# Bank waits moved to their tiles, and two norms' transposes set between halves of products, in a two-block transformer kernel

## The reference

```python
# first block
h = h + mixed                       # mixed = concat(...) @ w_out
z = rms_norm(h, ffn_gain) @ w_ff1   # 1024 -> 4096
h = h + square(relu(z)) @ w_ff2     # 4096 -> 1024
# second block
h = rmsnorm(x, norm_mix) * (1 + sc1) + sh1
proj = h @ w_in                     # 1024 -> 8192, then rope, retention, differential attention
x = x + g1 * (merged @ w_out)
x = x + g2 * hierarchical_moe(...)  # 32 experts
```

## Time and profile before

| | |
|---|---|
| median of 3 runs | 1199.39 us |
| the profiled execution's own time | 1197.58 us |
| its span, first to last instruction | 1195.8 us |
| mean granted TensorE clock | 0.987 of full |
| VectorE / ScalarE busy | 566.8 us (47%) / 477.0 us (40%) |
| chain that ended last | TensorE 89%, VectorE 3%, ScalarE 3% |
| DMA queue time, share of 16 engines | 70.6% |

### The profile page before, as it was taken

The page is one execution under the profiler, slowest core; times in us unless marked ns, Lnnn a source line. Parts: engine busy times, 40 slices in busy tenths (PEclk is TensorE's granted clock), DMA queues, the critical chain, the costliest instruction groups (busy, mean ns, idle before and its releaser), DMA issues.

```text
span 1195.8 us, 19252 instructions
## 1 busy us (share of the span) xinstructions
PE 1157.4 (97%) x8093; PEld 890.7 (74%) x8093; DVE 566.8 (47%) x860; ACT 477.0 (40%) x790; POOL 16.2 (1%) x32
## 2 busy tenths in 40 slices
PE   7989999999999999999999999999999999999995
PEld 6968888799988878878888787666666666666663
DVE  5688344677674377477564644222222222222222
ACT  5566133454443354563556524322222232332222
POOL 3000000000000000000000000000000000000000
PEclk9889999999999999999999999999999999999998
DMA  9743769255455555454444479999999999999992
GB/s 318 240 141 129 260 248 344 86 211 198 158 209 188 171 160 184 141 185 145 162 141 141 165 321 373 411 430 428 429 428 429 429 430 429 429 427 429 429 429 105
DMA packets 79823, 332.08 MB, mean 278 GB/s; under 512 B 4236, under 2 KB 6607, under 8 KB 63231
## 3 DMA queue, kind: packets, MB, share of 16 engines
q1 hardware_dynamic: 78356, 328.43, 70.6%
q0 software_dynamic: 1088, 2.34, 0.8%
q10 hardware_dynamic: 298, 0.11, 0.0%
HBM read 329.82 MB, written 1.05 MB: 277 GB/s over the span
## 4 chain that ended last, share of the span: by engine, by line
PE 89%; DVE 3%; ACT 3%; issue 2%; DMA 1%; SPq 1%; ACTq 0%; DVEq 0%
PE bank L1036 19%; PE bank L434 13%; PE bank L436 13%; PE bank L435 13%; PE bank L1055 10%; PE bank L1028 5%; PE bank L552 3%; PE bank L427 2%; DMA ring<-in_w_in 1%; PE bank L1075 1%; DVE arena L1822 1%; PE bank L1076 1%; ACT arena_r L1235 1%; PE bank L1043 1%; SPq L2496 0%
## 5 line engine op out<-in xcount | busy, mean ns | idle before, releaser
L1739 DVE TENSOR_TENSOR ring_r<-ring,arena_r 128x2048 fp32r<-128x2048 f32 x93 | 212.3, 2291 | 164.6 <-ACT arena_r L1235 163.8
L1235 ACT ACTIVATE arena_r<-ring 128x2048 fp32r<-128x2048 f32 x93 | 177.6, 1917 | 201.1 <-PE bank L436 189.8
L436 PE MATMUL bank<-arena_r,actT_r 128*128 128x512 f32 (+1 forms) x400 | 157.3, 393 | 0.0
L434 PE MATMUL bank<-arena_r,tok_r 128*128 128x512 f32 (+1 forms) x368 | 146.6, 398 | 3.3 <-issue 2.3
L435 PE MATMUL bank<-ring_r,tok_r 128*128 128x512 f32 (+1 forms) x368 | 143.4, 390 | 0.0
L2328 DVE TENSOR_TENSOR arena<-bank,arena 64x512 f32<-64x512 f32 x64 | 44.1, 689 | 180.5 <-PE bank L1055 179.8
L434 PE MATMUL bank<-tok_r,arena_r 128*128 128x256 f32 x352 | 99.4, 282 | 2.8 <-DVE ring_r L1751 1.9
L1206 ACT ACTIVATE arena<-bank 128x512 f32<-128x512 f32 (+5 forms) x132 | 57.5, 464 | 110.4 <-PE bank L1043 46.8
L435 PE MATMUL bank<-actT_r,arena_r 128*128 128x256 f32 x352 | 99.6, 283 | 0.0
L436 PE MATMUL bank<-tok_r,ring_r 128*128 128x256 f32 x352 | 98.1, 279 | 0.0
L434 PE MATMUL bank<-arena_r,arena_r 128*128 128x512 f32 x224 | 89.3, 399 | 0.6 <-DVE ring_r L1739 0.6
(11 more groups left out here) (404 smaller groups left out, 1680.3 us busy)
## 6 DMA issues: line engine op xcount, KB each, us to landing
ring<-in_w_in SPq DMA_DIRECT2D x22, 2048.0 KB, 8.9
ring<-in_w_exp_gate SPq DMA_DIRECT2D x21, 2048.0 KB, 20.4
arena<-in_w_exp_down SPq DMA_DIRECT2D x21, 2048.0 KB, 21.4
arena<-in_w_exp_up SPq DMA_DIRECT2D x21, 2048.0 KB, 23.6
ring<-in_w_ff SPq DMA_DIRECT2D x16, 2048.0 KB, 8.8
ring<-in_w_ada SPq DMA_DIRECT2D x12, 2048.0 KB, 8.9
ring<-in_w_exp_up SPq DMA_DIRECT2D x11, 2048.0 KB, 22.0
arena<-in_w_exp_gate SPq DMA_DIRECT2D x11, 2048.0 KB, 22.0
```

The source lines that it names most:

```text
L434: mm(o, l[0], r[0], start=start, stop=False)
L436: return mm(o, l[1], r[0], start=False, stop=stop)
L1235: A(hi, w, ACT.Copy).then_inc(S["w_high"], 1)
L1739: TT(half(i, ringR)[0], w, hi.bitcast(fp32), ALU.subtract).then_inc(S["w_rest"], 1)
```

## The change

Three things change. `split_product` begins a tile's bank just ahead of that tile's first half, so the wait for tile 1's bank stands behind tile 0's first 12 matmuls. In the second norm the tile 1 transposes of banks 0 and 1 stand between the halves of quarter (1,1), and z0 is cut in four groups of 12 matmuls: f = 0 with k = 0 to 3, then the tile 1 transposes of banks 2 and 3, f = 1 with k = 0 to 3, then, after banks 2 and 3 are read, both with k = 4 to 7. It now waits for the rests of banks 0 and 1 together, and of banks 2 and 3 together. In the third norm the last chunk of `w_ff2` is done bank by bank in full, the tile 0 transposes stand ahead of y3, both halves of p0_0 follow y3, and the tile 1 transposes follow p0_0; on VectorE diagonal 0 moves ahead of addition 2, and the rests of tile 0's banks 0 and 1 ahead of addition 3.

```diff
--- before.py
+++ after.py
@@ -450,10 +450,12 @@
                 return i
 
             def split_product(kind, c, name, acts=(aH, aL), between=None):
-                bks = [begin(f"{name}{t}") for t in range(T)]
+                bks = []
                 for h in range(2):
                     w = wait_split(kind, c, h)
                     for t in range(T):
+                        if h == 0:
+                            bks.append(begin(f"{name}{t}"))
                         i = part(bks[t], acts, t, h, w)
                         if h == 1:
                             end(i, f"{name}{t}")
@@ -718,14 +720,17 @@
             assert adas[0] == 12
             mod_turn(3)
 
-            def out_product(c, t):
+            def out_product(c, t, between=None):
                 for j in range(2):
                     wait_read(pe, f"oT{t}{j}")
                 bk = begin(f"mo{c}{t}")
                 for h in range(2):
                     i = part(bk, (oH, oL), t, h, wait_split("wout", c, h))
-                    if t == 1 and h == 0:
-                        i.then_inc(S["half_used"], 1)
+                    if h == 0:
+                        if t == 1:
+                            i.then_inc(S["half_used"], 1)
+                        if between:
+                            between()
                 end(i, f"mo{c}{t}")
                 last_job[place[("wout", c)]] = f"mo{c}{t}"
 
@@ -743,23 +748,39 @@
             bks = [begin(f"n2T{j}") for j in range(4)]
             for j in range(4):
                 x_transposes(bks[j], j, 0)
-            out_product(1, 1)
-            for j in range(4):
-                if j % 2 == 0:
-                    pe.wait_ge(S["x1_new"], 3 + j // 2)
-                end(x_transposes(bks[j], j, 1), f"n2T{j}")
+
+            def turn_x1(hh):
+                pe.wait_ge(S["x1_new"], 3 + hh)
+                for j in (2 * hh, 2 * hh + 1):
+                    end(x_transposes(bks[j], j, 1), f"n2T{j}")
+
+            out_product(1, 1, lambda: turn_x1(0))
+
+            def ff1_part(bk, f, ks, hi, rest):
+                fs = slice(f * P, (f + 1) * P)
+                for k in ks:
+                    i = mm3(bk[:, f * 256:(f + 1) * 256], (hi[:, k, fs], rest[:, k, fs]),
+                            (aH[:, k, :], aL[:, k, :]), f == 0 and k == 0, f == 1 and k == KT - 1)
+                return i
+
             for c in range(8):
                 for hh in range(2):
                     n = f"z{2 * c + hh}"
                     hi, rest = wait_split("ff1", c, hh)
                     bk = begin(n)
-                    for f in range(2):
-                        fs = slice(f * P, (f + 1) * P)
-                        for k in range(KT):
-                            if c == 0 and hh == 0 and f == 0 and k % 2 == 0:
-                                wait_read(pe, f"n2T{k // 2}")
-                            i = mm3(bk[:, f * 256:(f + 1) * 256], (hi[:, k, fs], rest[:, k, fs]),
-                                    (aH[:, k, :], aL[:, k, :]), k == 0, k == KT - 1)
+                    if c == 0 and hh == 0:
+                        for j in (0, 1):
+                            wait_read(pe, f"n2T{j}")
+                        ff1_part(bk, 0, range(4), hi, rest)
+                        turn_x1(1)
+                        ff1_part(bk, 1, range(4), hi, rest)
+                        for j in (2, 3):
+                            wait_read(pe, f"n2T{j}")
+                        ff1_part(bk, 0, range(4, 8), hi, rest)
+                        i = ff1_part(bk, 1, range(4, 8), hi, rest)
+                    else:
+                        for f in range(2):
+                            i = ff1_part(bk, f, range(KT), hi, rest)
                     end(i, n)
                 last_job[place[("ff1", c)]] = n
             bks = [begin(f"y{j}") for j in range(4)]
@@ -770,7 +791,7 @@
                 return mm3(bks[j][:, :], (zTR[:, 4 * c + f, ts], zTLR[:, 4 * c + f, ts]),
                            (hi[:, f % 2, hs], rest[:, f % 2, hs]), c == 0 and f == 0, c == 7 and f == 3)
 
-            for c in range(8):
+            for c in range(7):
                 pe.wait_ge(S["z_done"], 2 * c + 2)
                 hi, rest = wait_split("ff2", c, 0)
                 for f in range(2):
@@ -778,17 +799,10 @@
                         i = ff2_part(c, f, j, hi, rest)
                 i.then_inc(S["half_used"], 1)
                 hi, rest = wait_split("ff2", c, 1)
-                if c < 7:
-                    for f in range(2, 4):
-                        for j in range(4):
-                            i = ff2_part(c, f, j, hi, rest)
-                    i.then_inc(S["ff2_used"], 1)
-                else:
+                for f in range(2, 4):
                     for j in range(4):
-                        for f in range(2, 4):
-                            i = ff2_part(c, f, j, hi, rest)
-                        end(i, f"y{j}")
-                    last_job[place[("ff2", 7)]] = "y3"
+                        i = ff2_part(c, f, j, hi, rest)
+                i.then_inc(S["ff2_used"], 1)
 
             def scaled_transposes(t):
                 pe.wait_ge(S["n3_diag"], t + 1)
@@ -809,13 +823,23 @@
                             (hi[:, k, :], rest[:, k, :]), a == 0, a == 7)
                 return i
 
-            scaled_transposes(0)
+            pe.wait_ge(S["z_done"], 16)
+            w = [wait_split("ff2", 7, h) for h in range(2)]
+            for j in range(4):
+                if j == 3:
+                    scaled_transposes(0)
+                for f in range(4):
+                    i = ff2_part(7, f, j, *w[f // 2])
+                    if j == 3 and f == 1:
+                        i.then_inc(S["half_used"], 1)
+                end(i, f"y{j}")
+            last_job[place[("ff2", 7)]] = "y3"
             w0 = wait_split("win2", 0, 0)
             bk = begin("p0_0")
             first_part(bk, 0, 0, w0)
-            scaled_transposes(1)
             w1 = wait_split("win2", 0, 1)
             end(first_part(bk, 0, 1, w1), "p0_0")
+            scaled_transposes(1)
             bk = begin("p0_1")
             first_part(bk, 1, 0, w0).then_inc(S["half_used"], 1)
             end(first_part(bk, 1, 1, w1), "p0_1")
@@ -2084,8 +2108,8 @@
                 dve.wait_ge(S[scale], t + 1)
                 TS(diag3[t], ident, rstd[:, t:t + 1], None, ALU.mult).then_inc(S[sem], 1)
 
-            def scaled_rest(t):
-                for j in range(4):
+            def scaled_rest(t, js=range(4)):
+                for j in js:
                     bk = wait_full(dve, f"n3T{t}{j}")
                     dve.wait_ge(S["n3_high"], 4 * t + j + 1)
                     whole = ropeO[:, j * 256:(j + 1) * 256]
@@ -2099,9 +2123,11 @@
 
             for j in range(3):
                 add_ff(j)
-            scaled_diag(0, "n3_rs", "n3_diag")
+                if j == 1:
+                    scaled_diag(0, "n3_rs", "n3_diag")
+            scaled_rest(0, range(2))
             add_ff(3)
-            scaled_rest(0)
+            scaled_rest(0, range(2, 4))
             scaled_diag(1, "n3_rs", "n3_diag")
             scaled_rest(1)
             w_rest(W2 + 2)
```

## The result

The changed kernel took **1191.8 us** (median of 7 runs, 1190.56 to 1194.83), the kernel before 1197.89 us on the same chip (7 runs, 1196.71 to 1201.48): a ratio of **0.995 (0.9934 to 0.9966)**. The forecast was 1199.0 us, within 1196.2 to 1201.2. It was wrong, by 7 us and on the fast side of its range. Of these, 1.5 us lie in the kernel before, which took 1197.89 us here and 1199.39 when the forecast was made; the difference was forecast at -0.3 us and came out at -6.1.

What follows compares the result with a forecast made beforehand. TensorE, busy 97% of the span, was taken as the bound. Terms of -3.79, +4.0 and -0.55 us summed to -0.3, giving 1199.0 us against the median of 1199.39, range 1196.2 to 1201.2.

Steps and rivals of the forecast that it cites:

- Part 1, -3.79: Ahead of product 8: asking for banks tile by tile removes a 2.36 us wait and 1.43 us of low clock.
- The clock's term: First steps of product 8: with the wait gone, the slow steps behind it go too, saving 1.43 us.
- The rival of the unmoved wait: At product 8: the "issue" wait is not the bank and stays; +3.5 us in all, 1202.8; chance 0.08.
- Part 2, waits, +2.41: Second norm and z0: waits of 2.76 and 1.3 us make z0 end 2.41 us later.
- Part 2, clock, +1.6: At z0: the clock falls behind the 2.76 us wait, costing 1.6 us, with ends 0 and 2.7.
- the rival that the clock holds: At z0: no clock fall, so the second norm costs only 2.41 us; -1.9 in all, 1197.5; chance 0.30.
- Part 3, -0.55: Third norm: idle time falls from 1.77 to 1.25 us, one 1.20 us wait staying ahead of p0_1.
- Sum, -0.3: Whole kernel: -3.79 + 4.0 - 0.55 gives -0.3 us, 1199.0 against the median.
- I count 1 for 1: Experts' part: loads and matmuls shift together, so a shift ahead of it reaches the end in full.
- within 0.2%: Whole kernel: the time stays the same to within 2.4 us; chance 0.67, against faster 0.20 and slower 0.13.

Runs made afterwards that it cites:

- e3: The kernel before with only the split_product edit (banks tile by tile): 1194.17 us, ratio 0.997 to the kernel before.
- e6: The changed kernel with the second norm and z0 of the kernel before: 1193.31 us, ratio 0.997 to the kernel before.
- e0: The changed kernel run again, line for line: 1196.01 us, ratio 0.9999 to the kernel before.
- e14: Second run of the kernel before with only the second norm and z0 changed: 1202.37 us, ratio 1.0028 to the kernel before.
- e7: The kernel before with only the second norm and z0 changed: 1199.6 us, ratio 0.9997 to the kernel before.
- e11: The changed kernel once more, line for line: 1195.24 us, ratio 0.9966 to the kernel before.
- e15: The changed kernel once more: 1196.62 us, ratio 0.9987 to the kernel before.
- e10: The kernel before with only the third norm changed: 1198.83 us, ratio 1.0002 to the kernel before.
- e1: The kernel before with one start and one stop flag per bank in ff1: 1197.7 us, ratio 0.9998 to the kernel before.
- e2: The changed kernel with two start and two stop flags put back in z1 to z15: 1197.15 us, ratio 0.9988 to the kernel before.
- e12: The kernel before with TensorE waiting ahead of each z1 to z15 until the z before it is read; no total time given.
- e13: The changed kernel with TensorE waiting ahead of each z1 to z15 until the z before it is read; no total time given.

## Why the prediction was wrong

**Part 1, -3.79.** Right in mechanism and size. "Issue" was the wait for tile 1's bank: with the bank asked for later no wait is left, in the changed kernel, e3 and e6, and the 2.31 to 2.33 us are there in each kernel without the edit. 2.33 us for 2.36. The clock's term came out at 1.42 us for 1.43 (1.4 to 1.6 over the profiles); but it is paid in 7 executions of 8, not always. The rival of the unmoved wait is out.

**Part 2, waits, +2.41.** Right: 2.75 and 1.10 to 1.20 us for 2.76 and 1.3. From the quarter's first half to z1 the kernels with the clock held take 2.5 us more than before (13.62 + 2.86 = 16.48 in e0, where 2.86 = 241.22 - 238.36 is from the first half's start to the transposes; before 13.95). The interleaving put four transposes between matmuls and made both groups wait for the last rest of a pair of banks, in place of waits bank by bank: 1.14 us of waiting became 3.9. e14 shows it in the time, e7 doesn't.

**Part 2, clock, +1.6.** The size was right, the reasoning was not. I put 2.76 us "on the side of the one that fell", as if there were a length above which the clock falls. The fall came in 2 profiles of 9 at 2.75 us, in 7 of 8 at 2.32, and in 24 streams of 28 at 2.54 to 2.57. The case with the largest share in what executions do was the rival that the clock holds, which had 0.30. The Trainium skill (TensorE: Matmul & The Clock Gate, Why this matters for your kernels) wants no idle gaps between bursts above a length that is more than all of these. By that none of them would have cost the clock; the trace agrees in 7 profiles of 9 at 2.75 us and disagrees in 7 of 8 at 2.32 and in 24 streams of 28.

**Part 3, -0.55.** 0.81 us less in the changed kernel, e0, e11 and e15 alike (99.12 to 99.15 us from the end of `w_ff1`'s product to p0_1), and in e10 0.76. The wait that remains is of the size that I counted: the 0.95 us of the bracket are the same before and after, and by the forecast's way of counting, from the transposes' start to p0_1, it is 436.87 - 433.97 = 2.90 us less 1.80, so 1.10 for 1.25. (By its own figures the forecast's gain was 1.77 - 1.25 = 0.52.) e10's time shows nothing of it, as it is well under the 0.2% that can be told.

**Sum, -0.3, and the range.** The failed step is the one that was not written: all that lies outside the three places was taken as the same from one execution to the next, "the sum is made against the profiled execution" and "I count 1 for 1". The profile of before had `w_ff1`'s product at its slow step. I used 0.12 us a step as the duration of such a matmul, and it is one of two values; the other is worth 4.0 us over 720 matmuls, more than any net effect of the change and most of the 5.6 us between the two spans. The clock ahead of the experts and at their end is a second such term, worth up to 2.8 and 1.7 us (e11 against e0), where "from 560 us on the products run without a gap" was read from no row.

The first comparison had luck with it: its seven times of the changed kernel are all below 1195, where the 36 later ones have a median of 1195.5 and reach 1202.65. By the straight line above, some 2.5 of the 3.6 us between the mean times go with the clock. How much the step gave is not shown, as only one of the seven runs was profiled. With that luck out, the change is worth 2 to 3 us, not 0.3. About 1 us of the forecast's error is the clock in part 2; what remains, another 1 to 2, is within what 43 runs with such a spread leave open. I can't exclude that one of the edits makes the fast step a little more frequent: it came in 4 of 8 whole profiles with part 2 and in 2 of 7 without.

The chances had "within 0.2%" (2.4 us) at 0.67; -3.0 lies beyond it, -2.4 and the sum of the parts on its edge. The range was too narrow by its own evidence: 3 runs of before, 2 us apart, were taken for the spread of the kernel, whose 120 runs here go from 1191.6 to 1202.1 us.

The version to keep is e6, the changed kernel with the second norm of before. On its chip it beat the kernel before (0.997) and had a median 2.7 us under the changed kernel's. Part 1 alone (e3) can't be told from it: their mean times differ by 0.2 us (-2.3 to +1.9).

## What to carry to other kernels

Before forecasting a change of a few us, compare the same untouched stretch in two profiles: if its matmuls per us or its granted clock differ, that scatter belongs in the range, and a comparison of seven runs can fall on one side of it. Interleaving helps where the work put in between is longer than the chain it covers; here 1.4 us of matmuls and four transposes stood before a chain of 3 us, and waiting for a pair of banks in place of one bank at a time moved the whole latency of the pair onto TensorE. An "issue" in front of a product whose two banks are asked for together is worth a look at who last read the second bank.

## What the hardware showed that I had not expected

- Back-to-back fp32r matmuls of 256 columns step at 0.1133 or at 0.1187 to 0.1189 us at full clock, and keep the value for hundreds of matmuls. Both occur in one execution, from the same code, with a share of about four in ten for the faster (11 of 30 broken streams, 6 of 15 whole ones). What picks it is open: not the start and stop flags (e1, e2), not the kernel's code (e6, e12, e13), not a fall of the clock ahead of it (e2 fast without one). Whether it is drawn at idle time or when the clock returns was not separated: of the four streams of e12 and e13 without a fall all were slow.
- The clock's fall behind 2.3 to 2.8 us of idle time is a matter of when, not only of how long: 24 of 28 at 2.54 to 2.57 us (and the first streams of e12 and e13, behind 3.60 and 4.31), 7 of 8 at 2.32, 2 of 9 at 2.75. Once fallen it stayed low for 14 to 17 matmuls of 0.213 us.
- By the Trainium skill (TensorE: Matmul & The Clock Gate, Part 1) a warm matmul steps at its columns divided by 2.4 GHz plus 2.5 ns, from which I estimate 0.109 us here. Both steps measured lie above it, by 4 and by 10 ns, so this stream is not at that floor in either.
